# Expert input of a decoder step: the two products with the high weight as one 512-column matmul, halves added by VectorE

## The chip, the cores and the metric

One Trainium2 chip, one core of it. The metric is the device time of one execution in microseconds, from the first to the last instruction on the slowest (here the only) core, as the median of the runs.

## What is computed

One layer of a hybrid decoder for 256 prompt tokens and 32 sample tokens (T = 288 together, D_MODEL = 2048): an input projection, three attention branches, their output projection, and then a layer of product-key experts. The change lies in that last part. Its reference, cut to what matters:

```python
def peer_ffn(xn, w_q, keys, u, v):          # 16384 experts, 8 heads, 16 picks a head
    q = (tb @ w_q).reshape(nt, PEER_HEADS, 2, PEER_DK)
    sc = jnp.einsum('thcd,hcnd->thcn', q, keys)
    # top 16 of each half, top 16 of the 256 pairs, softmax: weights g, expert numbers eid
    act = jax.nn.gelu(jnp.einsum('thkd,td->thk', u[eid], tb), approximate=False)
    return jnp.einsum('thk,thkd->td', (g * act), v[eid])
```

## The kernel before

For 256 of the 288 tokens (DENSE) the kernel doesn't gather experts. It multiplies all 16384 rows of u with the tokens, takes gelu, weighs the result with a table that is zero where a token didn't pick the expert, and multiplies with v. The last 32 tokens (SPARSE) go by gathered rows: dots with rows of u, sums with rows of v.

Every product of f32 numbers is made of three products in a reduced 32-bit format: x = x_high + x_low and w = w_high + w_low, and the product is w_high x_high + w_high x_low + w_low x_high, all three summed in the same bank.

The stage of the change is the expert input, in `peer` (from line 2360). The 128 experts of a block are the columns of the weights, the contraction runs over D_MODEL in KT = 16 tiles of 128. BLOCKS = 128 blocks go through these steps, all engines at work on different blocks:

- DMA loads the block of u, 1 MB, half of it issued by SyncE once both halves of an earlier block are turned (`load_u`), half by ScalarE behind `high` (`load_quadrants`, line 2451). There are two buffers, and three from block 30 on (THIRD_FROM).
- VectorE transposes it in two half blocks (`turn`, line 2795). `half_block` does one such transpose and the dots of gathered rows due then. In the first third, half blocks are dealt out between the instructions of the top-16 search for three groups of tokens (`top16`, `worked`), in proportion to their cost. Later, `hot_rows` (lines 2905 and 2910) makes the operands of the weight table between the two halves.
- ScalarE copies each half to uT_high (`high`, line 2672), once PE is done with the block before last. GpSimd subtracts it for uT_low (`low_halves`, line 2645) and issues the gathers.
- PE runs `hidden(s, c)` (from line 2538): for each of the 16 tiles the high weight with x_high (line 2545) and with x_low (line 2546), then, after four-matmul pieces of the weight table (`spread`, line 2581), for each tile the low weight with x_high (line 2552). All 48 matmuls have 256 columns and sum into the first half of bank 4 or 5, by turns. The first one waits for `gelu_ready` of the block before last, which frees the bank.
- ScalarE takes gelu from the bank into a ring of four buffers (`gelu`, line 2681). SyncE stores it to DRAM (`store_gelu`, line 2480), three blocks behind the turned block.

The orders on each engine are written out by hand and all its instructions are in that order: a wait stops what is queued behind it. ScalarE does in its loop over m: `high(m + 1)`, what is due of the picks and of the weight table, `gelu(m)`. At blocks 44 and 64 PE turns picks and waits for ScalarE's copy of them. `after(n)` in a wait is a semaphore's start value plus n.

Behind block 127 comes the output stage (`four`, `output`, lines 2612 to 2614): 128 blocks of v, 24 matmuls of 512 columns each. VectorE weighs the gelu rows (`weigh`, line 2938, 2945, 2947) and makes the low half of v (`low_v`, line 2952). The gelu rows and the table come back from DRAM by `load_weights` (lines 2475 and 2476), the second of them behind the last `store_gelu`.

## Time and profile before

| what | value |
|---|---|
| runs | 3119.73, 3121.1, 3122.23 us; median 3121.1 us |
| span of the profiled execution (no other time is given for it) | 3122.4 us |
| instructions | 52270 |
| PE busy | 2977.9 us, 95% |
| weight loads (beside PE) | 2779.4 us, 89% |
| VectorE busy | 1834.2 us, 59% |
| ScalarE busy | 1266.4 us, 41% |
| GpSimd busy | 1023.3 us, 33% |
| DMA | 698.31 MB, mean 224 GB/s |

A matmul's duration is modelled and overlaps the next one's, so paces are read from starts, or from how many start in a stretch. Starts are us from the span's start. PE is the matmul row, PEld the weight loads, DVE is VectorE, ACT ScalarE, POOL GpSimd, SP SyncE; a q behind the name is the engine's queue where it issues DMAs. "banks" are the PSUM banks. The clock is the share of TensorE's full clock that was granted.

### The profile page before, as it was taken

How to read it: one execution, taken by the hardware profiler on the slowest of the kernel's cores; microseconds unless marked ns; L12 is line 12 of the kernel's file. 1: busy time of each engine (PE TensorE's matmuls, PEld its weight loads, DVE VectorE, ACT ScalarE, POOL GpSimd, SP SyncE). 2: the span in 40 equal slices, each digit the busy share in tenths (PEclk: the TensorE clock that was granted, in tenths of full speed). 3: DMA queues.
4: the chain of work that ended last, by engine and by line, in shares of the span. 5: the costliest groups of instructions: out<-in, count | busy, mean ns of one | idle time of the engine just before them, and what ended most of it. 6: DMA issues, size and time to landing. Idle time of an engine off the chain costs nothing. (4 is left out here: it accounts for less than half of the span.)

```text
span 3122.4 us, 52270 instructions
## 1 busy us (share of the span) xinstructions
PE 2977.9 (95%) x20998; PEld 2779.4 (89%) x20998; DVE 1834.2 (59%) x2568; ACT 1266.4 (41%) x1399; POOL 1023.3 (33%) x549
## 2 busy tenths in 40 slices
PE   7999999898989979998999999999999999999997
PEld 6999999887888869997999999999998888888886
DVE  5444444375221145645468999877784577767764
ACT  5322233345533454433344444445553333333332
POOL 0000000134644420024057889777775011111000
PEclk9999999999999989999999999999999999999999
DMA  7555544575675646666768999999999788888754
GB/s 233 182 167 167 166 161 161 166 226 163 186 250 182 222 141 190 200 206 168 153 159 191 241 242 236 255 287 289 273 266 358 257 319 312 304 297 306 289 199 174
DMA packets 449277, 698.31 MB, mean 224 GB/s; under 512 B 30981, under 2 KB 345765, under 8 KB 421582
## 3 DMA queue, kind: packets, MB, share of 16 engines
q1 hardware_dynamic: 398622, 553.81, 57.7%
q10 hardware_dynamic: 41296, 75.53, 8.8%
q0 software_dynamic: 9216, 67.11, 5.7%
q8 instruction: 84, 1.38, 0.2%
q14 instruction: 59, 0.48, 0.0%
HBM read 629.24 MB, written 63.72 MB: 222 GB/s over the span
## 5 line engine op out<-in xcount | busy, mean ns | idle before, releaser
L2645 POOL TENSOR_TENSOR peer_uT_low<-peer_uT,peer_uT_high 128x1024 fp32r<-128x1024 f32 x256 | 615.6, 2427 | 255.3 <-ACT peer_uT_high L2672 254.7
L1054 POOL TENSOR_TENSOR gate_low<-gate_raw,gate_high 128x512 fp32r<-128x512 f32 x192 | 257.9, 1368 | 878.9 <-ACT gate_high L1005 878.5
L2545 PE MATMUL banks<-x_high,peer_uT_high 128*128 128x256 f32 x2048 | 493.1, 283 | 5.1 <-ACT peer_picks_T L2704 5.1
L2546 PE MATMUL banks<-x_low,peer_uT_high 128*128 128x256 f32 x2048 | 489.1, 280 | 0.0
L2545 PEld LDWEIGHTS banks<-x_high,peer_uT_high 128*128 128x128 f32 x2048 | 386.6, 189 | 5.8 <-ACT peer_uT_high L2672 2.9
L2546 PEld LDWEIGHTS banks<-x_low,peer_uT_high 128*128 128x128 f32 x2048 | 385.8, 188 | 0.0
L257 PE MATMUL banks<-x_high,win_high 128*128 128x288 f32 (+1 forms) x1312 | 349.3, 296 | 0.0
L258 PE MATMUL banks<-x_low,win_high 128*128 128x288 f32 (+1 forms) x1312 | 348.7, 295 | 0.0
L227 ACT ACTIVATE win_high<-win_raw 128x2048 fp32r<-128x2048 f32 x84 | 160.8, 1914 | 332.5 <-DVEq L220 319.2
L2672 ACT ACTIVATE peer_uT_high<-peer_uT 128x1024 fp32r<-128x1024 f32 x256 | 260.5, 1053 | 59.2 <-DVE peer_uT L2795 58.8
L2795 DVE STREAM_TRANSPOSE peer_uT<-peer_u 128x1024 f32<-128x1024 f32 x192 | 233.8, 1229 | 82.9 <-DMA peer_u<-in_peer_u_dram 56.8
L2552 PE MATMUL banks<-x_high,peer_uT_low 128*128 128x256 f32 x2048 | 263.8, 282 | 0.0
L233 DVE TENSOR_TENSOR win_low<-win_raw,win_high 128x2048 fp32r<-128x2048 f32 x84 | 192.4, 2291 | 116.8 <-ACT win_high L227 116.8
L2552 PEld LDWEIGHTS banks<-x_high,peer_uT_low 128*128 128x128 f32 x2048 | 250.2, 189 | 0.0
L258 PEld LDWEIGHTS banks<-x_low,win_high 128*128 128x128 f32 x1312 | 247.2, 188 | 0.1
L257 PEld LDWEIGHTS banks<-x_high,win_high 128*128 128x128 f32 x1312 | 246.5, 188 | 0.3
L1068 PE MATMUL banks<-x_high,gate_high 128*128 128x288 f32 x768 | 222.7, 311 | 22.2 <-POOL gate_low L1054 15.0
L2653 POOL DMA_INDIRECT peer_area<-in_peer_v_dram,peer_expert_row x32 | 61.9, 1935 | 472.7 <-DVE peer_area L2920 471.7
L2720 ACT ACTIVATE peer_uT_high<-peer_u 128x2048 fp32r<-128x2048 f32 x64 | 122.8, 1919 | 227.8 <-PE banks L2614 201.3
L1069 PE MATMUL banks<-x_low,gate_high 128*128 128x288 f32 x768 | 213.7, 300 | 0.0
L2612 PE MATMUL banks<-x_high 128*128 128x512 f32 x512 | 201.0, 393 | 12.2 <-DVE x_low L2952 12.2
L2720 ACT ACTIVATE x_high<-peer_area 128x2048 fp32r<-128x2048 f32 x64 | 122.7, 1919 | 219.2 <-PE banks L2614 217.0
(395 smaller groups left out, 6502.0 us busy)
## 6 DMA issues: line engine op xcount, KB each, us to landing
win_raw<-in_w_in_dram SPq DMA_DIRECT2D x38, 2048.0 KB, 8.1
peer_u<-in_peer_v_dram SPq DMA_DIRECT2D x64, 1024.0 KB, 5.6
peer_area<-in_peer_v_dram SPq DMA_DIRECT2D x64, 1024.0 KB
gate_raw<-in_w_in_dram SPq DMA_DIRECT2D x96, 512.0 KB, 5.0
peer_u<-in_peer_u_dram SPq DMA_DIRECT2D x192, 256.0 KB
peer_u<-in_peer_u_dram ACTq DMA_DIRECT2D x192, 256.0 KB
w_raw<-in_w_up_ret_dram SPq DMA_DIRECT2D x8, 2048.0 KB, 9.0
w_raw<-in_w_out_dram SPq DMA_DIRECT2D x8, 2048.0 KB, 8.4
```

The source lines that it names most:

```text
L257: pe.matmul(out, w, xh[:, k, :], start=(k == 0), stop=False)
L258: pe.matmul(out, w, xl[:, k, :], start=False, stop=False)
L1054: pool.tensor_tensor(self.low[:, p % 2, c, :, :], self.raw[:, p % 4, :, c * P:(c + 1) * P], self.high[:, p % 2, c, :, :], ALU.subtract).th ...
L1068: pe.matmul(out, high, self.xh[:, 4 * q + k, :], start=(q == 0 and k == 0), stop=False)
L1069: pe.matmul(out, high, self.xl[:, 4 * q + k, :], start=False, stop=False)
L2545: pe.matmul(out, UH[:, c, k, :], XH[:, k, 0:DENSE], start=(k == 0), stop=False)
L2546: pe.matmul(out, UH[:, c, k, :], XL[:, k, 0:DENSE], start=False, stop=False)
L2552: last = pe.matmul(out, UL[:, c, k, :], XH[:, k, 0:DENSE], start=False, stop=(k == KT - 1))
L2645: pool.tensor_tensor(UL[:, m % 2, part, :], UT[:, m % 2, part, :], UH[:, m % 2, part, :], ALU.subtract).then_inc(low, 1)
L2672: act.activation(UH[:, m % 2, part, :], UT[:, m % 2, part, :], ACT.Copy).then_inc(uT_high, 1)
L2720: act.activation(VH[n % 4], V[n % 4], ACT.Copy).then_inc(v_high, 1)
L2795: dve.transpose(UT[:, m % 2, b * HALF:(b + 1) * HALF, :].rearrange("p c (E e) -> p E c e", E=4), u_block(m)[:, :, cols].rearrange("p E (c ...
```

## The change

The two products with the high weight become one matmul of 512 columns. x_high and x_low now lie in one tensor, and the matmul's moving operand is 256 columns of each. Its result is the whole bank: in the first half the product with x_high, in the second that with x_low. The low weight's product is still summed into the first half.

So the halves have to be added before gelu. ScalarE copies the second half to SBUF (`cross`), VectorE adds the first half from the bank and writes the ring of gelu rows (`add_cross`), and ScalarE takes gelu in place. VectorE's sum of block m stands in `half_block`, right ahead of the second transpose of block m + 3 (HIDDEN_BEHIND); the last three sums stand behind all of VectorE's work of the stage, ahead of the first `weigh`. The wait for the stored gelu row moves from ScalarE to that sum. PE's wait for a free bank is now for the sum of the block before last. ScalarE does gelu one block later: its loop ends with `cross(m)`, `gelu(m - 1)`.

```diff
-            XH = tensor(right, "right", "x2_high", [P, KT, T], F32R)
-            XL = tensor(right, "right", "x2_low", [P, KT, T], F32R)
+            X2 = tensor(right, "right", "x2", [P, 2, KT, T], F32R)
+            XH, XL = X2[:, 0], X2[:, 1]
...
-TURNS_AHEAD, GATHERS_AHEAD = 2, 4
+TURNS_AHEAD, GATHERS_AHEAD, HIDDEN_BEHIND = 2, 4, 3
...
+        CROSS = st.sb("cross_products", [P, 2, DENSE])
...
                     out = PS[:, 4 + c, 0:DENSE]
-                    pe.wait_ge(gelu_ready, after(m - 1))
+                    parts = PS[:, 4 + c, :].rearrange("p (x t) -> p x t", x=2)
+                    pe.wait_ge(hidden_added, after(m - 1))
                     for k in range(KT):
                         if k % HALF == 0:
                             pe.wait_ge(uT_high, after(m * 2 + k // HALF + 1))
-                        pe.matmul(out, UH[:, c, k, :], XH[:, k, 0:DENSE], start=(k == 0), stop=False)
-                        pe.matmul(out, UH[:, c, k, :], XL[:, k, 0:DENSE], start=False, stop=False)
+                        pe.matmul(parts, UH[:, c, k, :], X2[:, :, k, 0:DENSE], start=(k == 0), stop=False)
...
+                def cross(m):
+                    act.wait_ge(hidden_done, after(m + 1))
+                    act.wait_ge(hidden_added, after(m - 1))
+                    act.activation(CROSS[:, m % 2, :], PS[:, 4 + m % 2, DENSE:2 * DENSE], ACT.Copy).then_inc(cross_copied, 1)
+
                 def gelu(m):
-                    act.wait_ge(hidden_done, after(m + 1))
-                    act.wait_ge(ge_stored[m % 4], after(16 * (m // 4)))
-                    act.activation(GE[:, m % 4, :], PS[:, 4 + m % 2, 0:DENSE], ACT.Gelu).then_inc(gelu_ready, 1)
+                    act.wait_ge(hidden_added, after(m + 1))
+                    act.activation(GE[:, m % 4, :], GE[:, m % 4, :], ACT.Gelu).then_inc(gelu_ready, 1)
...
-                    gelu(m)
+                    cross(m)
+                    if m:
+                        gelu(m - 1)
+                gelu(BLOCKS - 1)
...
+                def add_cross(m):
+                    dve.wait_ge(cross_copied, after(m + 1))
+                    dve.wait_ge(ge_stored[m % 4], after(16 * (m // 4)))
+                    dve.tensor_tensor(GE[:, m % 4, :], PS[:, 4 + m % 2, 0:DENSE], CROSS[:, m % 2, :], ALU.add).then_inc(hidden_added, 1)
+
                 def half_block():
                     h = next(halves)
+                    if h % 2 == 1 and h // 2 >= HIDDEN_BEHIND:
+                        add_cross(h // 2 - HIDDEN_BEHIND)
                     turn(h)
...
+                for m in range(BLOCKS - HIDDEN_BEHIND, BLOCKS):
+                    add_cross(m)
                 weigh(0)
```

## Rows read from the trace of the kernel before

**Rows 1.** The page, first section: busy us, share of the span, instructions

```profile
PE 2977.9 (95%) x20998; PEld 2779.4 (89%) x20998; DVE 1834.2 (59%) x2568; ACT 1266.4 (41%) x1399; POOL 1023.3 (33%) x549
```

**Rows 2.** The chain of waits, 1660 to 1690 us: start us, us, what

```profile
1667.30 1.88 PE banks L2552 x16
...
1684.24 1.88 PE banks L2552 x16
```

**Rows 3.** Groups by shape, 1580 to 2410 us: count, busy us, mean ns, idle before

```profile
L2645 POOL TENSOR_TENSOR peer_uT_low<-peer_uT,peer_uT_high 128x1024 fp32r<-128x1024 f32 x256 | 615.6, 2427 | 255.3 <-ACT peer_uT_high L2672 254.7
...
L2795 DVE STREAM_TRANSPOSE peer_uT<-peer_u 128x1024 f32<-128x1024 f32 x192 | 233.8, 1229 | 82.9 <-DMA peer_u<-in_peer_u_dram 56.8 <-POOL peer_uT_low L2645 25.5
```

**Rows 4.** Windows of VectorE, blocks 16-30, 30-44: us, busy, clock, DMA share, GB/s

```profile
1678.00:1757.00 79.00, 67.36 (x174) 1.00 0.86 207
1757.00:1832.00 75.00, 72.97 (x125) 1.00 0.97 254
```

**Rows 5.** VectorE's waits, 1584 to 1678, 1678 to 1757, 1832 to 1909: us, times, longest

```profile
DVE peer_uT L2795 <- DMA peer_u<-in_peer_u_dram: 13.7, 7, 7.5
...
DVE peer_uT L2795 <- DMA peer_u<-in_peer_u_dram: 13.8, 8, 2.8
...
DVE peer_uT L2795 <- POOL peer_uT_low L2645: 9.5, 6, 4.4
```

**Rows 6.** Windows, PE alone, output stage: us, busy (matmuls), clock, DMA, GB/s

```profile
2500.00:2600.00 100.00, 100.00 (x442) 1.00 0.84 307
```

**Rows 7.** Groups by shape of VectorE and ScalarE, whole span: count, busy, mean ns

```profile
L2070 DVE TENSOR_TENSOR up_mix<-banks,up_gates 128x288 f32<-128x288 f32 x16 | 7.3, 455 | 41.8 <-ACT up_gates L2058 34.1 <-PE banks L263 7.6
...
L559 ACT ACTIVATE Z<-banks 128x256 f32<-128x256 f32 x8 | 3.1, 383 | 40.3 <-PE banks L668 40.3
```

**Rows 8.** Transposes from 1580 us on (count, ns), and timeline near 1707 us

```profile
L2795 DVE STREAM_TRANSPOSE peer_uT<-peer_u x42: 1198/1232/1248, 1584.0 to 1707.4; 128x1024 f32<-128x1024 f32 x42
...
1706.66 2.04 PE L2552 MATMUL banks<-x_high,peer_uT_low 128*128 128x256 f32 x16
...
1707.38 1.25 DVE L2795 STREAM_TRANSPOSE peer_uT<-peer_u 128x1024 f32<-128x1024 f32 x1
```

**Rows 9.** Timeline near block 37: start us, us, engine, line, count

```profile
1797.01 2.04 PE L2552 MATMUL banks<-x_high,peer_uT_low 128*128 128x256 f32 x16
...
1801.79 1.24 DVE L2795 STREAM_TRANSPOSE peer_uT<-peer_u 128x1024 f32<-128x1024 f32 x1
```

**Rows 10.** Timeline near block 59

```profile
1924.52 2.04 PE L2552 MATMUL banks<-x_high,peer_uT_low 128*128 128x256 f32 x16
...
1929.30 1.24 DVE L2795 STREAM_TRANSPOSE peer_uT<-peer_area 128x1024 f32<-128x1024 f32 x1
```

**Rows 11.** Timeline near block 83, VectorE and PE: in brackets the idle time before

```profile
2077.74 1.25 DVE L2795 STREAM_TRANSPOSE peer_uT<-peer_area 128x1024 f32<-128x1024 f32 x1 [6.00 <-DMA peer_area<-in_peer_u_dram]
...
2084.84 1.24 DVE L2795 STREAM_TRANSPOSE peer_uT<-peer_area 128x1024 f32<-128x1024 f32 x1
...
2083.11 1.16 PE L2581 MATMUL banks<-peer_keys_T_and_hot_rows 128*128 128x128 f32 x8 [2.78 <-DVE peer_keys_T_and_hot_rows L2910]
2084.02 0.36 PE L2545 MATMUL banks<-x_high,peer_uT_high 128*128 128x256 f32 x1
```

**Rows 12.** Timeline at the end of the stage, 2381 to 2411 us

```profile
2381.68 4.75 POOL L2645 TENSOR_TENSOR peer_uT_low<-peer_uT,peer_uT_high 128x1024 fp32r<-128x1024 f32 x2 [0.90 <-ACT peer_uT_high L2672]
...
2385.56 1.49 DVE L2938 TENSOR_TENSOR peer_area<-peer_area 128x256 f32<-128x256 f32 x2 [8.21 <-DMA peer_area<-peer_weights]
...
2389.49 2.04 PE L2552 MATMUL banks<-x_high,peer_uT_low 128*128 128x256 f32 x16
...
2392.82 0.48 SPq L2476 DMA_DIRECT2D peer_area<-peer_weights  x1
...
2408.75 0.77 PE L2612 MATMUL banks<-x_high 128*128 128x512 f32 x1 [6.32 <-DVE x_low L2952]
...
2410.17 0.63 PE L2612 MATMUL banks<-x_high 128*128 128x512 f32 x1
```

More of the change, by code:

```diff
@@ L336, in decoder_step_kernel @@
                 output_projection(nc, G, MH, ML, hT, area, moved, keys_loaded, gain_loaded, w_out, w_q)
-            XH = tensor(right, "right", "x2_high", [P, KT, T], F32R)
-            XL = tensor(right, "right", "x2_low", [P, KT, T], F32R)
+            X2 = tensor(right, "right", "x2", [P, 2, KT, T], F32R)
+            XH, XL = X2[:, 0], X2[:, 1]
             norm_and_queries(nc, G, area, hT, XH, XL, moved, spilled, gain_loaded, w_q)
             left.close()
-            peer(nc, G, area, XH, XL, spilled, keys_loaded)
+            peer(nc, G, area, X2, spilled, keys_loaded)
 def constants(const):
@@ L2357, in spread_at, with peer @@
     return range(spread_before(m), spread_before(m + 1))
-def peer(nc, G, area, XH, XL, spilled, keys_loaded):
+def peer(nc, G, area, X2, spilled, keys_loaded):
     A, PS, ident, C, S, O = (G[k] for k in ("A", "PS", "ident", "C", "S", "O"))
+    XH, XL = X2[:, 0], X2[:, 1]
     GR = 2 * PEER_HEADS
@@ L2431, in peer @@
             "second_ready", "first_ready", "placed", "weights_ready", "weights_stored")
-        turned, uT_high, low, hidden_done, gelu_ready, iota_ready, xrows_moved = st.sems(
-            "turned", "uT_high", "uT_low", "hidden_done", "gelu_ready", "iota_ready", "xrows_moved")
+        turned, uT_high, low, hidden_done, cross_copied, hidden_added, gelu_ready, iota_ready, xrows_moved = st.sems(
+            "turned", "uT_high", "uT_low", "hidden_done", "cross_copied", "hidden_added", "gelu_ready", "iota_ready", "xrows_moved")
         u_loaded = st.sems(*(f"u_loaded{r}" for r in range(4)))
```

## The prediction

> **What bounds the kernel now.** The page's first section gives the order of the engines: PE is busy in 95% of the span [rows 1]. The change touches one stage, the expert input, whose 128 blocks run from 1588 us to 2391 us, so I read that stage. The chain of waits shows it as PE alone: a block's low products come every 5.647 us (1667.30 to 1684.24 is three blocks [rows 2]), which is 48 matmuls at 117.65 ns with no gap. So PE is the bound, and what PE saves is saved, as long as its suppliers keep up. They are close behind. The groups of the stage give the cost of the suppliers per block [rows 3]: POOL 256 x 2.43 us, that is 4.86 us a block; VectorE two transposes of 1.23 us, and beside them all the top-16 picking, in the first 66 blocks. By the windows, VectorE is busy in 67.4 of 79 us, then in 73.0 of 75 us [rows 4]. Its waits are for the DMA of u up to block 30 (13.7, 13.8 us) and only from block 46 on for POOL (9.5 us) [rows 5]. So for the first 44 blocks nothing holds VectorE back but its own work and its loads. That it costs no time now is because it runs ahead of PE by a lead that is allowed to shrink.
>
> **The matmuls.** Removed are 2048 pairs of 256-column matmuls with the same weights, added 2048 matmuls of 512 columns. A pair takes 2 x 117.65 = 235.3 ns [rows 2]. The next stage issues matmuls of just this width with new weights each: 442 in 100 us, 226.2 ns [rows 6]. The moving operand is now read in two pieces of 256; nothing in the trace shows that as a cost, and I take 226.2. Saving 9.1 ns x 2048 = 18.6 us, or 0.145 us a block. Bounds: 235.3 ns (no saving) and 213.3 ns (512 columns at the granted 2.4 GHz, 45 us). The row is the same width and type, so I take it.
>
> The trace's 117.65 ns is 11 ns above 256 columns at the granted 2.4 GHz. The Trainium skill (TensorE: Matmul & The Clock Gate, section "Wait — 56ns, not 53.3ns?") states a fixed 2.5 ns over the columns for every warm matmul; by that a pair would go from 218.3 to 215.8 ns and the change could save 5 us only. The rows at either width disagree with it.
>
> **ScalarE.** Per block a copy of 128x256 out of a bank is added; such a copy takes 383 ns [rows 7]. Gelu stays, now from SBUF. ScalarE's queue then has, after a block's end on PE: copy, gelu of the block before, the two high halves. The high halves come 0.4 us later, and POOL's halves behind them. POOL's halves for block 127 end at 2381.68 + 4.75 = 2386.43, and PE starts the low products at 2389.49 [rows 12]: 3.1 us of cover for 0.4. Where PE waits for ScalarE itself, at the two hand-overs of the picks, the 0.4 us shows: +0.8 us.
>
> **VectorE.** 128 additions of 256 columns with one operand in a bank. The nearest row is a sum of 288 columns with one operand in a bank, 455 ns [rows 7]; by columns alone 256 take 404 ns. I take 0.42 us between the two. In the first 66 blocks it has no room for them, see above.
>
> **The new wait, which decides.** Before, PE started block m once gelu of block m-2 was done, by ScalarE, which is always there in time. After, it needs the sum of block m-2, and that stands in VectorE's queue right ahead of the second transpose of block m+1. So PE's block B-1 can't start until VectorE has come to the second transpose of block B, plus 0.42 for the sum and 0.1 to wake: half a microsecond. Before, it only had to have block m itself turned. I count transposes on VectorE, and PE's blocks in the same way by their 16 low products, to see where it stood. The 42nd transpose (block 20, second half) starts at 1707.38; the low products of PE's block 19 start at 1706.66 and take 1.88, so with 5.65 a block it started at 1702.9: VectorE is 4.5 us too late for the new order [rows 8]. By the same count, block 37 (76th) at 1801.79 against block 36 on PE at 1798.9: 2.9 us too late [rows 9]. Block 59 (120th) at 1929.30 against block 58 at 1926.4: again 2.9 us [rows 10]. PE will be stopped in each, so its shift P against before is at least D + 3.4 at the last two, where D is VectorE's own delay by the new sums.
>
> D: between blocks 3 and 37 there are 35 sums, 14.7 us if all count, 0 if all fall into its DMA waits of 27 us. Loads are issued behind the second transpose, and u has two buffers up to block 30, so every other block a sum is inside the loop that the load closes, and the other one falls into the wait; from block 30 VectorE is full. So (27 / 2 + 8) x 0.42 = 9, less what the waits early on hide, about 3: D = 6. P = 9.4 at block 36. From there PE recovers 0.145 a block as long as it isn't stopped, and VectorE, which waits for POOL there, is tied to it: P = 7.5 at block 52, D with it. Then seven sums (2.9) without a wait ahead of block 59: D = 10.5, P = 14.
>
> From block 58: 70 blocks x 0.145 = -10; the hand-over of the picks is in the 0.8 above. In the second half (blocks 66 on) VectorE has a lead of more than 0.6 us nearly everywhere, enough for the sum. One pattern breaks it: a late load of u holds VectorE's queue 6.0 us, and the second transpose of block 83 comes at 2084.84, 0.8 us after PE's block 82 started at 2084.02 [rows 11]. The sum now stands behind that load: +1.3 there, and about 1 each for the two other times that the weight table is stored, +3.
>
> A stop of PE also costs clock. After 2.78 us idle [rows 11] and after 6.32 us idle [rows 12] the matmuls behind it come at half the pace (three of 512 columns in 1.42 us, 2408.75 to 2410.17). Two of the new stops are 4 us long in one piece; I put 1 us on each, since PE waits on VectorE there anyway: +2.
>
> **End of the stage.** Before, weigh, split and subtraction of the first v block ran on VectorE beside PE's block 127 (2385.56 and after), and PE went on at once [rows 12]. Now they are queued behind the sum of block 127: some 0.9 + 1.49 + 0.43 + 0.69 + 2.29, about 6 us after PE's end. That gap is mostly not new: before PE stood for 6.32 us two v blocks later, for the second load of weights, which is issued after the last gelu (2392.82). The last gelu now ends 1.2 us later, and the two v blocks in front of it fit in the same time. +1.3.
>
> Sum on the profiled execution: P 14 + 0.8 - 10 + 3 + 2 + 1.3 = +11. Its span is 3122.4 us, no other time is given for it, and it stands 1.3 above the median of the runs, 3121.1. So 3132 us for the median. A difference under 0.2% (6 us) I count as none, about what a measurement of this kernel can tell.
>
> **The rivals.**
> (a) VectorE has room: the sums fall into the DMA waits and D is 0. Then P is 3.4 at block 36, 1.5 at block 52, 4.9 at block 58 and the total is about +1: 3122. For it: 27 us of waits. Against: 73.0 of 75 busy. With D between 0 and 3 it stays within 0.2%.
> (b) The order isn't binding at all, because a PE that is stopped once lets VectorE lead from there on, and wide matmuls pay in full: -18.6 + 1.3 + 3, 3107. It needs VectorE to keep 5.5 us a block with sums in it, so that after the first stop of 4.5 us none follows: some -10, 3111.
> (c) Worse than forecast: loads decide. All 35 sums count (D = 14.7, P = 18 at block 36), and the stores of the gelu rows, which leave a block later, meet the weight table in SP's queue, so that VectorE's sum waits for a row of the buffer: +18 to +30, 3139 to 3151. It decides where a store takes more than two blocks.
> (d) The wide matmul isn't faster than its pair: 235.3 instead of 226.2 ns, everything else as forecast: 3149, or 3135 where VectorE bounds the first half anyway. The rows of the next stage speak against it. The Trainium skill's rule above would be near this case.
>
> **How the numbers follow.** Forecast (+5 to +16) 0.45, (a) 0.25, (b) 0.17, (c) 0.08, (d) 0.05. The likeliest case alone is 3126 to 3138. Of the forecast's cases a small part is inside 0.2%, so faster 0.18, same 0.27, slower 0.55. The range leaves out a tenth on either side: 3108 to 3146.
>
> **What would show it.** Right: PE's matmuls of 512 columns 226 ns apart in a stretch without stops, 5.50 us a block; PE idle in front of the first matmul of a block with VectorE's sum as the releaser, most in blocks 18 to 44 and 56 to 62, some 20 to 30 us in all; VectorE almost without idle time there; the last blocks of the stage with hardly any. Wrong: the sum of 256 columns well under 0.4 us; blocks at 5.50 us already between 20 and 40 (then (a) or (b)); blocks spaced over 5.64 us without a wait (then (d)). The forecast falls if PE's idle time on that wait is under 12 us.

## The result, and the profile after

The changed kernel takes 3166.09 us (median of four runs, 3163.62 to 3170.87), the kernel before in the same comparison 3120.41 (3119.63 to 3122.23). The ratio is 1.0146 with a 95% interval of 1.0131 to 1.0160: slower by 46 us. The profiled execution took 3167.94 us, its span is 3166.2 us, 43.8 over the 3122.4 of before. The forecast was 3132 us, with a range of 3108 to 3146. The sign is right, the size is not: the measured time lies 20 us above the range.

The first section of the page, busy us, share of the span and instructions [rows 1]:

```profile
PE 2983.6 (94%) x18950; PEld 2689.3 (85%) x18950; DVE 1871.0 (59%) x2696; ACT 1302.1 (41%) x1527; POOL 1022.0 (32%) x549
```

PE has 2048 matmuls less. VectorE has 128 instructions and 37 us more: 128 sums at 0.41 us are 52 us, and the rest of its work sums to 15 us less in this profile. The engines' totals say little; the waits say where the time is. First PE's waits in the stage, 1580 to 2470 us of the changed kernel: engine, line, waited for, us in total, times, longest:

```profile
PE banks L2583 <- ACT peer_area L2717: 21.6, 3, 8.4
PE banks L2548 <- DVE peer_gelu L2813: 16.8, 10, 2.9
PE banks L2548 <- ACT peer_picks_T L2710: 5.7, 2, 3.0
PE banks L2614 <- DVE peer_uT_low L2968: 5.2, 1, 5.2
PE banks L2614 <- DVE x L2968: 4.9, 1, 4.9
...
```

The same view of the kernel before, 1580 to 2420 us:

```profile
PE banks L2612 <- DVE x_low L2952: 6.3, 1, 6.3
PE banks L2581 <- DVE peer_keys_T_and_hot_rows L2910: 5.2, 3, 2.8
...
PE banks L2581 <- ACT peer_area L2711: 1.1, 2, 0.9
```

The second line of the changed kernel's is the wait that the forecast counted on: the first matmul of a block (L2548) waits for VectorE's sum (L2813). The first line is the surprise. At three places the weight table's matmuls (L2583) wait for ScalarE's L2717, a step that used to cost 1.1 us. L2717 takes a finished piece of the table out of its bank (`keep`), and at those three places a new group of tokens begins, so that the old table must have gone to DRAM first.

To see where the shift arises I took the start of each block on PE in both profiles. The stage itself begins 3.2 us earlier in the changed kernel's profile, a variation of what lies ahead of it, so I count from the stage's first block:

| stretch | shift gained, us | what it is |
|---|---|---|
| blocks 0 to 66 | +17.0 | eight stops for the sum (15.2, of which 13.0 are idle time), a block at half the clock behind three of them (5.0), the picks (0.6), less 66 faster blocks (4.0) |
| blocks 66 to 127, ordinary blocks | -2.7 | the wide matmul, 0.06 us a block, less small stops |
| blocks 81 to 83, 95 to 99, 108 to 112 | +5.4, +7.5, +7.9 | the three hand-overs of the weight table |
| blocks 124 to 126 | +4.3 | a stop for the sum, which is queued behind a late load of u, and a block at half the clock |
| from block 127 on | +7.6 | the change to the output stage |
| total | +47.0 | |

**The stops for the sum.** Of the 16.8 us of waits for the sum in the stage, most lie ahead of block 66; the same view from 1580 to 1970 us:

```profile
PE banks L2548 <- DVE peer_gelu L2813: 13.0, 8, 2.9
```

The timeline of PE in the changed kernel, start, us, instruction, and in brackets the idle time ahead of it:

```profile
1708.04 5.54 PE L2548 MATMUL banks<-x,peer_uT_high 128*128 128x512 f32 x16 [2.87 <-DVE peer_gelu L2813]
1713.41 2.05 PE L2554 MATMUL banks<-x,peer_uT_low 128*128 128x256 f32 x16
1715.30 3.86 PE L2548 MATMUL banks<-x,peer_uT_high 128*128 128x512 f32 x16
1719.00 2.05 PE L2554 MATMUL banks<-x,peer_uT_low 128*128 128x256 f32 x16
```

Two things are to be seen. PE stood for 2.87 us, and then 16 matmuls of 512 columns took 5.54 us instead of 3.86. The granted clock tells why; the windows of PE over a part of each of the two blocks (us, busy and matmuls, clock, DMA share, GB/s):

```profile
1708.10:1711.50 3.40, 3.40 (x10) 0.64 0.38 42
1715.40:1718.90 3.50, 3.50 (x17) 1.00 1.06 240
```

The first mean, 0.64, is a mixture of the two levels, 1.2 and 2.4 GHz. It happened behind the three longest of the eight stops, ahead of blocks 19, 34 and 56 (2.87, 2.59 and 2.42 us idle); with it they cost 4.7, 4.4 and 4.2 us.

Not every such stop has a halved clock behind it. PE also waits for the picks, ahead of block 44. Here is that stop in the changed kernel, and then in the profile of the experiment table_first, whose program does the same up to this point:

```profile
1857.55 3.97 PE L2548 MATMUL banks<-x,peer_uT_high 128*128 128x512 f32 x16 [3.00 <-ACT peer_picks_T L2710]
```

```profile
1860.18 5.52 PE L2548 MATMUL banks<-x,peer_uT_high 128*128 128x512 f32 x16 [3.00 <-ACT peer_picks_T L2710]
```

The same 3.00 us of idle time, and behind it 16 matmuls in 3.97 us at a granted clock of 1.00 once, in 5.52 us at 0.67 the other time. So the length of a stop doesn't decide it, and a single profile can differ from the next by such blocks.

**The pace between stops.** The block is read between the starts of its low products, 1713.41 to 1719.00: 5.59 us, where [rows 2] had 5.65 and the forecast 5.50. The low products themselves keep 117.65 ns, so the wide matmul takes 231.6 ns, not 226.2.

**A hand-over.** Three views of the first one belong together. SyncE's queue in the changed kernel:

```profile
2070.87 0.34 SPq L2482 DMA_DIRECT2D gelu<-peer_gelu  x1
2071.26 0.95 SPq L2497 DMA_DIRECT2D peer_weights<-peer_area  x2
...
2076.45 0.34 SPq L2482 DMA_DIRECT2D gelu<-peer_gelu  x1
2076.84 1.36 SPq L2497 DMA_DIRECT2D peer_weights<-peer_area  x2
```

And in the kernel before:

```profile
2052.62 0.43 SPq L2480 DMA_DIRECT2D gelu<-peer_gelu  x1
2053.09 0.92 SPq L2495 DMA_DIRECT2D peer_weights<-peer_area  x2
...
2059.61 0.44 SPq L2480 DMA_DIRECT2D gelu<-peer_gelu  x1
2060.09 0.98 SPq L2495 DMA_DIRECT2D peer_weights<-peer_area  x2
```

In either, the store of the table follows a store of a gelu row by 0.4 us: it is queued behind it in SyncE's order of instructions. The gelu row now comes one block later, and so does the table, although no edit names the table. With the 13 us shift of this place taken off, the first table store is at 2058.3 instead of 2053.1, the second at 2063.8 instead of 2060.1. The chain of waits of the changed kernel follows it on:

```profile
2076.84 0.86 SPq L2497
...
2077.74 22.76 DMA peer_weights<-peer_area
...
2100.59 1.03 ACT peer_area L2717
...
2101.76 2.04 PE banks L2583 x8
```

ScalarE waited 11.09 us for this store ahead of L2717, where before it waited 2.73 us, and PE stood for 8.42 us ahead of 2101.76 behind it. The store's own time in flight is longer too: 22.8 us from the end of its issue, and before 17.8, from the end of its issue at 2061.07 to ScalarE's copy at 2078.83.

**The end of the stage.** VectorE in the changed kernel:

```profile
2428.11 0.42 DVE L2813 TENSOR_TENSOR peer_gelu<-banks,peer_cross_products 128x256 f32<-128x256 f32 x1 [5.16 <-ACT peer_cross_products L2683]
...
2430.43 4.48 DVE L2968 TENSOR_TENSOR peer_uT_low<-peer_u,peer_uT_high 128x2048 fp32r<-128x2048 f32 x2
2446.12 0.76 DVE L2954 TENSOR_TENSOR peer_area<-peer_area 128x256 f32<-128x256 f32 x2 [11.21 <-DMA peer_area<-peer_weights]
```

PE's block 127 ends at 2427.67. The work for the first v block stands behind the last sum, and PE starts the output stage 5.2 us later. Two v blocks on it stops again for the second load of weights, 4.90 us, until 2450.42. From the end of block 127 to there are 22.75 us; before, from 2391.57 to 2408.75 [rows 12], 17.2. The load is issued 1.8 us after the end instead of 1.25, and is in flight 16.25 us instead of 11.61.

### The profile page after: what moved, and what is told of

The parts are those of the page before. It is cut to its first block, busy times and chain, and to the rows that moved or that the text cites. A ratio compares the mean times of both kernels' runs of the same rounds, so it can differ in the third digit from the quotient of the medians.

```text
span 3166.2 us, 48558 instructions
## 1 busy us (share of the span) xinstructions
PE 2983.6 (94%) x18950; PEld 2689.3 (85%) x18950; DVE 1871.0 (59%) x2696; ACT 1302.1 (41%) x1527; POOL 1022.0 (32%) x549
## 4 chain that ended last, share of the span: by engine, by line
PE 40%; DMA 5%; DVE 3%; issue 1%; ACT 1%; POOL 0%; ACTq 0%; SPq 0%; DVEq 0%
PE banks L2548 11%; PE banks L2614 7%; PE banks L2616 7%; PE banks L2615 7%; PE banks L2554 6%; DMA peer_u<-in_peer_u_dram 2%; PE banks L2583 2%; DMA peer_weights<-peer_area 1%; DVE peer_uT L2804 1%; DMA peer_area<-peer_weights 1%; DMA peer_area<-in_peer_v_dram 0%; POOL peer_uT_low L2647 0%; DVE x L2968 0%; PE banks L2567 0%; PE banks L2635 0%
## 5 line engine op out<-in xcount | busy, mean ns | idle before, releaser
L2548 PE MATMUL banks<-x,peer_uT_high 128*128 128x512 f32 x2048 | 508.9, 401 | 22.6 <-DVE peer_gelu L2813 16.8
L2548 PEld LDWEIGHTS banks<-x,peer_uT_high 128*128 128x128 f32 x2048 | 382.5, 192 | 106.4 <-issue 15.1
L2554 PEld LDWEIGHTS banks<-x,peer_uT_low 128*128 128x128 f32 x2048 | 257.2, 189 | 8.7
L2554 PE MATMUL banks<-x,peer_uT_low 128*128 128x256 f32 x2048 | 263.7, 282 | 0.0
L2726 ACT ACTIVATE x<-peer_area 128x2048 fp32r<-128x2048 f32 x64 | 122.8, 1919 | 226.6 <-PE banks L2616 218.9
L2614 PE MATMUL banks<-x 128*128 128x512 f32 x512 | 201.7, 394 | 11.0 <-DVE x L2968 11.0
L2614 PE MATMUL banks<-peer_uT_high,peer_act_high 128*128 128x512 f32 x512 | 200.7, 392 | 5.2 <-DVE peer_uT_low L2968 5.2
L2615 PE MATMUL banks<-x 128*128 128x512 f32 x512 | 201.4, 393 | 0.0
```

The costliest lines, as they stand in the source:

```text
L2548: pe.matmul(parts, UH[:, c, k, :], X2[:, :, k, 0:DENSE], start=(k == 0), stop=False)
L2554: last = pe.matmul(out, UL[:, c, k, :], XH[:, k, 0:DENSE], start=False, stop=(k == KT - 1))
L2614: pe.matmul(out, high, VH[slot][:, cols], start=first, stop=False)
L2615: pe.matmul(out, rest, VH[slot][:, cols], start=False, stop=False)
L2726: act.activation(VH[n % 4], V[n % 4], ACT.Copy).then_inc(v_high, 1)
```

## The experiments

Shifts are again counted from the stage's first block, on the profiles; medians and ratios are those of the runs beside the kernel before. "Hand-overs" are the three of the weight table.

### The wide matmul alone

Only the matmul is changed; the bank's second half, the product with x_low, is not added, and this product is left out of the output. Everything else is as before.

```diff
-  pe.matmul(out, UH[:, c, k, :], XH[:, k, 0:DENSE], start=(k == 0), stop=False)
-  pe.matmul(out, UH[:, c, k, :], XL[:, k, 0:DENSE], start=False, stop=False)
+  pe.matmul(parts, UH[:, c, k, :], X2[:, :, k, 0:DENSE], start=(k == 0), stop=False)
```

> The change's wide matmul alone, on the kernel before: the 512-column matmul into the whole bank, and then gelu of the first half as before, by ScalarE, with the waits and the queues of before. Left out: the product of the high weight with x_low. Theory 'two pieces': the moving operand in two pieces of 256 costs about 5 ns a matmul, so a pair of 235.3 ns becomes one of 231.6 ns as in the changed kernel, 3.7 x 2048 = 7.6 us less than before: 3113 us, no stops of PE in the picks. Rival 'disturbed': the matmul is as fast as those of the output stage (226.2 ns), and in the changed kernel the new reads of the banks by ScalarE and VectorE slowed it: 18.6 us less, 3102 us.

Measured: 3123.66 against 3123.32 us, ratio 0.9998 (0.9987 to 1.0009). No gain is seen, and the interval has no room for the 7.6 us that were expected. Its timeline gives the pace without any sum in the kernel:

```profile
1882.58 3.86 PE L2548 MATMUL banks<-x,peer_uT_high 128*128 128x512 f32 x16
1886.28 2.05 PE L2554 MATMUL banks<-x,peer_uT_low 128*128 128x256 f32 x16
1888.16 3.86 PE L2548 MATMUL banks<-x,peer_uT_high 128*128 128x512 f32 x16
```

1882.58 to 1888.16, 5.58 us a block as in the changed kernel: 231.6 ns belong to the matmul. And the 0.06 us a block that are left don't arrive in the first half: PE, now faster, has to wait for halves that were there in time before, and longer for the picks. Its waits in the stage:

```profile
PE banks L2548 <- ACT peer_picks_T L2706: 7.8, 2, 5.4
...
PE banks L2548 <- ACT peer_uT_high L2674: 2.9, 2, 2.6
```

It stands 2.6 us at 1712 us and 5.4 instead of 2.7 for the picks, and behind both the clock was halved (eight wide matmuls in 3.38 us instead of 2.02, then 16 in 5.33 instead of 3.86). The shift is +5.7 at block 66, where the matmuls alone would give -4.0. From there to block 127 it falls to +0.6: in the second half the saving does arrive. The end is at +2.9, and this profile is 4 us above the median of its runs.

### Why 231.6 ns: one piece, address, bank

The first two runs start from mm_alone: the high weight is multiplied with 512 other, adjacent columns of x_high, so that both of its products are replaced; the second differs from the first in where the columns start. The third, in the kernel before, orders the output stage's matmuls by the weight, so that each goes to another bank than the one before it. This also names one weight four times in a row, but the weight loads stay one per matmul. In this order:

```diff
+  pe.matmul(PS[:, 4 + c, :], UH[:, c, k, :], xh[:, k * DENSE:k * DENSE + 2 * DENSE], start=(k == 0), stop=False)
...
+  pe.matmul(PS[:, 4 + c, :], UH[:, c, k, :], xh[:, k % 8 * 512:k % 8 * 512 + 512], start=(k == 0), stop=False)
...
+  for weight, v, begin, end in ((high, VH, first, False), (rest, VH, False, False), (high, VL, False, last)):
+      for j in range(4):
+          ins = pe.matmul(PS[0:r, 4 * i + j, :], weight, v[slot][:, j * 512:(j + 1) * 512], start=begin, stop=end)
```

> As the run before it, but the moving operand is 512 adjacent columns (of x_high alone, so the products are of other columns). Theory 'two pieces': 226 ns a matmul, 3102 us, 11 us less than with two pieces. Rival: the two pieces cost nothing and something else makes 231.6 ns in this stage (the weights' place, the u loads): same time as the run before it, 3113 us.

> As mm_one_piece, but the 512 columns start at multiples of 512 columns of the same tensor (2 KB apart, as the v rows in the output stage) instead of multiples of 256; the products are of other columns. Theory 'address': the pace of 232 ns comes from where the moving columns start; now 226.5 ns. Rival 'same bank': 16 matmuls in a row sum into one bank, against three in the output stage; still 231 to 233 ns.

> The kernel before with the output stage's 24 matmuls of 512 columns per block in another order: all four banks with one weight, then the next weight, so that no two matmuls in a row sum into the same bank. For the pace of the wide matmul: 16 in a row into one bank take 231 to 233 ns apart in the expert input, three in a row 226.5 ns here. Theory 'same bank': a matmul behind one into the same bank starts later; alternating banks take 216 to 222 ns, up to 30 us less: 3095 us. Rival: it is not the bank, 226.5 ns as before, 3121 us.

Measured: mm_one_piece 3129.93 against 3123.32 us, ratio 1.0012 (1.0001 to 1.0024), 233.3 ns; mm_steps, a single run, 3124.13 us, 233.3 ns; output_by_bank 3123.45 against 3123.19 us, ratio 1.0005 (0.9995 to 1.0015), its pace as in [rows 6], 442 in 100 us. The timeline of mm_one_piece:

```profile
1883.77 3.89 PE L2548 MATMUL banks<-x,peer_uT_high 128*128 128x512 f32 x16
1887.50 2.03 PE L2554 MATMUL banks<-x,peer_uT_low 128*128 128x256 f32 x16
```

1883.77 to 1887.50 are 3.73 us for 16. The operand in two pieces is not what costs 5 ns, nor its start address, and in the output stage staying in a bank doesn't make a matmul slower. What does stays open. Within a block of the changed kernel the starts lie 225 to 237 ns apart, by nearly the same pattern over the 16 tiles in most blocks; mm_alone has this pattern too.

### The place of the wait alone

No sum; VectorE only passes a semaphore on in the place where the sum would stand, and PE waits for that.

```diff
+  pe.wait_ge(passed, after(m - 1))
...
+  if h % 2 == 1 and h // 2 >= 3:
+      dve.wait_ge(gelu_ready, after(h // 2 - 2))
+      dve.sem_inc(passed, 1)
```

> The kernel before, and PE waits for VectorE's place in its queue as in the changed kernel: VectorE raises a semaphore ahead of the second transpose of block m+3, once gelu of block m is done, and PE starts block m+2 only then. No sum, no wide matmul, no change in SyncE's queue. Theory 'place': PE stops near blocks 19, 35 and 57 where VectorE trails, at least 4.5 us in all and 1.6 us for the clock after each stop, and PE, at its pace of before, recovers none of it: +6 to +8 us by block 66, some 2 to 4 more at the late loads: 3130 us. Rival 'price': it is the sums that cost the time in the first half, the place alone costs under 3 us: 3123 us.

Measured: 3127.77 against 3123.32 us, ratio 1.0006 (0.9997 to 1.0016). In the profile the shift is +3.4 at block 66, +8.6 at block 127, +9.1 at the end; the runs show less: the medians are 4 us apart, the ratio says 2 us, and its interval includes none. The stop is ahead of block 19, where the forecast's count put it, and 1.6 us long; it is the only one on this wait. Of the +3.4, 1.4 us are a block at half the clock behind the stop for the picks, a stop that the kernel before has as well. The rest of the shift comes at the weight table's hand-overs, where the wait for `keep` is 5.8 us instead of 1.1. The order by itself is cheap as long as VectorE's work doesn't grow.

### The price of the sums alone

First with both operands in SBUF, because no bank is free of other use at that time; nobody reads the result.

```diff
+  SPARE = st.sb("spare", [P, 2, DENSE])
...
+  if h % 2 == 1 and h // 2 >= 3:
+      dve.tensor_tensor(SPARE[:, 0, :], SPARE[:, 1, :], SPARE[:, 1, :], ALU.add).then_inc(spared, 1)
```

> The kernel before, and VectorE does one more sum of 256 columns at the place where the changed kernel has it, on a spare buffer that nobody reads or waits for. Theory 'price': VectorE has no room in the first 44 blocks, so the transposes come later by up to 6 us and PE stops for ScalarE's high halves near blocks 20 and 36: +3 to +10 us, 3129 us. Rival 'fits': the sums fall into the waits for loads: within 1 us of before.

Measured: 3177.31 against 3124.27 us, ratio 1.0170 (1.0153 to 1.0187), more than the whole change. It is not a test of the price, since the sum is not the same instruction any more. Its group in the stage (count, busy us, mean ns, idle before):

```profile
L2808 DVE TENSOR_TENSOR peer_spare<-peer_spare 128x256 f32<-128x256 f32 x125 | 133.2, 1065 | 0.3
```

1065 ns instead of 408. The timeline of VectorE and of GpSimd shows the longest one:

```profile
1906.91 7.15 DVE L2808 TENSOR_TENSOR peer_spare<-peer_spare 128x256 f32<-128x256 f32 x1
...
1906.67 7.10 POOL L2645 TENSOR_TENSOR peer_uT_low<-peer_uT,peer_uT_high 128x1024 fp32r<-128x1024 f32 x3
```

The sum stands about as long as three subtractions of GpSimd in a row, 1906.67 to 1913.77, and ends 0.3 us behind them. The Trainium skill (SBUF — State Buffer, section "Who interferes with whom") says that a VectorE instruction with two SBUF inputs contends with a GpSimd instruction that reads SBUF, while one with at most one SBUF input, outside VectorE's two-port modes, doesn't. This case agrees, by these rows and by the next run, where the mean is 406 ns instead of 1065.

So the same again with one operand in a bank (the constant iota, read from PSUM in two pieces of 128):

```diff
+  dve.tensor_tensor(SPARE[:, 0, :].rearrange("p (x n) -> p x n", x=2), PIOTA.unsqueeze(1).to_broadcast([P, 2, P]), SPARE[:, 1, :].rearrange("p (x n) -> p x n", x=2), ALU.add).then_inc(spared, 1)
```

> The kernel before, and at the place where the changed kernel has its sum VectorE adds 256 columns of a bank (the iota that lies there) to a spare buffer; nobody reads the result or waits for it. It differs from sums_alone in one thing: one operand is in a bank, as in the changed kernel, and not both in SBUF, where the sums took 1.07 us on average and up to 7 us behind a subtraction of GpSimd. Theory 'shared way to SBUF': these take 0.39 to 0.42 us each, as in the changed kernel, and then 'price' decides: VectorE comes later in the first 66 blocks, +3 to +10 us, 3129 us. Rival 'fits': 0 to 1 us.

Measured: 3140.15 against 3124.66 us, ratio 1.0051 (1.0039 to 1.0063). Group and waits of PE in the stage:

```profile
L2809 DVE TENSOR_TENSOR peer_spare<-banks,peer_spare 128x256 f32<-128x256 f32 x125 | 50.7, 406 | 0.5 <-DVE peer_picks L2894 0.4
```

```profile
PE banks L2545 <- ACT peer_picks_T L2704: 9.3, 2, 6.0
...
PE banks L2545 <- ACT peer_uT_high L2672: 4.3, 6, 2.6
```

406 ns is the price of the change's sum (408). The shift is +15.8 at block 66, +19.2 at block 127, +20.2 at the end. Here no new wait exists: PE stops because the picks come later (6.0 us in one stop, 2.7 before) and because the transposed halves do. Of the 26 us of sums up to block 66 some 16 arrived, in spite of VectorE's 27 us of DMA waits [rows 5]. A part of the 16 is clock: behind the two stops for the picks a block took 8.2 and 8.3 us from start to start, where the same blocks took 5.75 before.

### Place and price together

The unread sum of sums_bank, behind a wait for gelu of the block whose sum it stands for, with PE waiting for it; the matmuls stay as before.

```diff
+  pe.wait_ge(spared, after(m))
...
+  dve.wait_ge(gelu_ready, after(h // 2 - 2))
```

> The kernel before with the unread bank sums of sums_bank and PE's wait for them as in the changed kernel, no wide matmul and nothing changed on SyncE. Theory 'parts add': the sums alone gave +15 us, the wait for the place alone +4 us by the runs (9 us by the profile of the stage), so +18 to +24 us, 3145 us. Rival 'interplay': a sum that is late and waited for costs more than both alone, +30 us or more, 3155 us.

Measured: 3148.66 against 3123.19 us, ratio 1.0078 (1.0065 to 1.0090). The shift is +22.4 at block 66, +28.8 at block 127, +27.7 at the end, against 9.1 + 20.2 = 29.3 for the two alone. By the profiles they add. By the medians the two alone are 4.5 and 15.5 us over the kernel before, 20.0 together, and this kernel is 25.5 over it, a little more than the 18 to 24 expected; so some microseconds that only the two together cost can't be excluded. Its stops are ahead of much the same blocks as the changed kernel's:

```profile
PE banks L2546 <- DVE peer_spare L2811: 12.9, 8, 4.8
PE banks L2582 <- ACT peer_area L2712: 5.3, 2, 3.8
```

Against it the changed kernel has 15.4 us more in the hand-overs (5.3 us of waiting for `keep` here, 21.6 there), 8.7 more from block 127 on and 3.6 more at block 124; it has 5.4 less up to block 66, and 3 less between, where its wide matmul counts.

### The stores one block later, alone

```diff
 def store_gelu(m):
-    sp.wait_ge(gelu_ready, after(m + 1))
+    sp.wait_ge(gelu_ready, after(min(m + 2, BLOCKS)))
```

> The kernel before with one wait changed: SyncE's store of a gelu row waits until the gelu of the next block is done, as it has to in the changed kernel. No sum, no wide matmul. Theory 'queue': the stores of the weight table are queued behind it on SyncE, so each of the three hand-overs of the table to the next token block comes a block (5.6 us) later, and PE, which before stood 2.8 us at the first of them, stands that much longer: +14 to +18 us, 3137 us. Rival 'load': those stops grew because VectorE's sum is queued behind late loads of u; then this kernel is as before, 3121 us.

Measured: 3139.02 against 3123.32 us, ratio 1.0046 (1.0029 to 1.0063). One number in a kernel that is otherwise the one before, and +16 us. SyncE's queue, where the second store of the table was at 2060.09 before (this profile's stage begins 1.1 us later), and PE's waits:

```profile
2063.98 0.34 SPq L2480 DMA_DIRECT2D gelu<-peer_gelu  x1
2064.37 2.49 SPq L2495 DMA_DIRECT2D peer_weights<-peer_area  x2
```

```profile
PE banks L2581 <- ACT peer_area L2711: 13.0, 3, 5.4
...
PE banks L2612 <- DVE x_low L2952: 4.8, 1, 4.8
...
PE banks L2612 <- DVE peer_uT_low L2952: 4.1, 1, 4.1
```

The shift is zero up to block 81, +9.9 at block 113, and +13.9 at the end: the three hand-overs and the end of the stage, with a second stop of 4 us there, and nothing else. 13.0 of the changed kernel's 21.6 us are reproduced. What the others need beside the late stores isn't shown by a run; the late VectorE is the likely part, since place_and_price has 5.3 us of this wait without late stores.

### The table ahead of the gelu row

The converse, in the changed kernel: SyncE stores the table first.

```diff
-    if m >= 3:
-        store_gelu(m - 3)
     k, r = divmod(m - SPREAD_FROM - SPREAD_ACTIVE - 2, SPREAD_SPAN)
     if 0 <= k < TOKEN_BLOCKS and r < 2:
         ...
+    if m >= 3:
+        store_gelu(m - 3)
```

> The changed kernel, with the two parts of the weight table's stores put ahead of the store of the gelu row in SyncE's loop; nothing else. Theory 'queue': the hand-overs of the table at blocks 81, 95 and 109 get back the block that they lost, 5 us and some clock each: 14 to 18 us less than the changed kernel, 3150 us, and PE's waits for ScalarE's copy of the table fall from 21.6 us to some 6. Rival 'load': those stops are late loads behind the table's stores, which stay: under 4 us less, 3163 us.

Measured: 3159.79 against 3124.27 us (3150.0 to 3163.47), ratio 1.0112 (1.0089 to 1.0135). The hand-overs fall from 20.8 to 6.0 us in the profile and the wait for `keep` from 21.6 to 6.4 us; the first half came out at +24 instead of +17 in that profile, though this edit changes nothing there (the stop ahead of block 13 is 4.6 us instead of 1.6, and a halved clock also follows it and both stops for the picks), and the runs spread over 13 us, so the net gain, 1.0112 against 1.0146, is some 11 us, under the 14 to 18 expected, and uncertain by several. The same edit in the kernel before:

> The kernel before, with only the order on SyncE changed: table stores ahead of the gelu row's store. There gelu is done by then, so theory 'queue' expects nothing or the time of one store's issue (0.5 us) on each hand-over: 0 to -2 us, 3121 us. If the stops at the hand-overs were bound by that order even before, -5 us.

Measured: 3123.83 against 3123.19 us, ratio 1.0001 (0.9992 to 1.0010). Before, the table wasn't late.

### The sum at another place

Half a block earlier on VectorE, ahead of the first transpose of block m + 3:

```diff
-  if h % 2 == 1 and h // 2 >= HIDDEN_BEHIND:
+  if h % 2 == 0 and h // 2 >= HIDDEN_BEHIND:
```

> The changed kernel with the sum of block m ahead of the first transpose of block m+3 instead of the second: half a block earlier in VectorE's queue, and in front of the wait for the load of u. Theory 'place': most of the eight stops go, 10 to 18 us less than the changed kernel, 3152 us; the three stops at the table's hand-over stay. Rival 'price alone': under 5 us less, 3163 us.

Measured: 3150.17 against 3124.66 us, ratio 1.0081 (1.0068 to 1.0095). That is 20 us less over the kernel beside it than the change has, more than the 10 to 18 expected. The stops for the sum fall to 9.0 us, the shift at block 66 to +11.4 from +17.0. The hand-overs shrink only a little: PE stands 7.51, 6.54 and 3.76 us there, instead of 8.42, 7.90 and 5.32. A whole block earlier (HIDDEN_BEHIND = 2):

> The changed kernel with VectorE's sum two blocks behind its transposes instead of three (HIDDEN_BEHIND = 2). PE's block then needs VectorE at the second transpose of that same block, a whole block later than now, but VectorE can't run further ahead than PE's last finished block. Theory 'place': the eight stops of PE before a sum (15 us, and 5 us of half clock) go; 12 to 20 us less than the changed kernel, 3150 us. Rival 'VectorE waits': the time that it now stands for PE's products comes back as later transposes and loads: 3166 us or more.

Measured: 3183.6 against 3124.66 us, ratio 1.0193 (1.0180 to 1.0207). PE's waits in the stage:

```profile
PE banks L2583 <- ACT peer_area L2717: 34.1, 13, 10.1
PE banks L2583 <- DVE peer_keys_T_and_hot_rows L2926: 8.1, 9, 1.7
...
PE banks L2548 <- DVE peer_gelu L2813: 6.0, 5, 2.2
```

The stops for the sum are nearly gone, 6.0 us, and the shift at block 66 is +13.5. But in the second half (1980 to 2440 us) VectorE now waits for ScalarE's copy of a block that PE has only just ended:

```profile
DVE peer_gelu L2813 <- ACT peer_cross_products L2683: 99.3, 45, 5.9
```

In the changed kernel this wait is 20.6 us there. What is queued behind it is the operands of the weight table, and PE stops for the table 22 times in all (13 and 9). Of the three places tried, half a block earlier is the best.

### A bank freed by ScalarE alone

ScalarE copies both halves out in one instruction, PE waits for that copy, and VectorE adds in SBUF, in its own time.

```diff
-  pe.wait_ge(hidden_added, after(m - 1))
+  pe.wait_ge(cross_copied, after(m - 1))
...
-  act.activation(CROSS[:, m % 2, :], PS[:, 4 + m % 2, DENSE:2 * DENSE], ACT.Copy).then_inc(cross_copied, 1)
+  act.activation(RING[:, a:b + 1:b - a, :], PS[:, 4 + m % 2, :].rearrange("p (x t) -> p x t", x=2), ACT.Copy).then_inc(cross_copied, 1)
...
-  dve.tensor_tensor(GE[:, m % 4, :], PS[:, 4 + m % 2, 0:DENSE], CROSS[:, m % 2, :], ALU.add).then_inc(hidden_added, 1)
+  dve.tensor_tensor(GE[:, m % 4, :], GE[:, m % 4, :], CROSS[:, m % 2, :], ALU.add).then_inc(hidden_added, 1)
```

> The changed kernel, but ScalarE copies both halves of the bank in one instruction (512 columns), the first into the ring of gelu rows, PE waits for that copy as it waited for gelu before, and VectorE adds in place from SBUF at the same place in its queue. The sum stays, PE's wait for VectorE's place is gone. Theory 'place with price': the eight stops before a sum (15 us in the profile of the changed kernel, and 5 us of half clock behind three of them) are gone and PE may trail VectorE as before; a stop or two for late high halves comes in their place: 12 to 18 us less, 3151 us. Rival 'price alone': VectorE's load is what stops PE, wherever PE waits: under 6 us less, 3162 us.

> Both of the last two edits together. If they are two separate causes, their gains add: some 30 us less than the changed kernel, 3135 us. If one only uncovers the other, the gain is that of the larger alone, 3150 us.

Measured: bank_freed 3216.88 against 3124.27 us, ratio 1.0305 (1.0288 to 1.0322); freed_table_first, with the table's store ahead as well, 3211.69 us, ratio 1.0280 (1.0263 to 1.0297). The 3151 and 3135 us expected are missed by 66 and 77 us, for a reason that neither theory nor rival had. PE's wait for the sum is gone, and the sum costs 3.5 times as much:

```profile
L2814 DVE TENSOR_TENSOR peer_gelu<-peer_gelu 128x256 f32<-128x256 f32 x128 | 183.1, 1431 | 12.0 <-ACT peer_gelu L2685 8.7 <-issue 3.0
```

128 x 1.02 us is 131 us more of VectorE, the engine that had no room. That is the behaviour of sums_alone, met by a design that looked better on paper.

### Half a block earlier and the table first

Both edits, sum_first_half and table_first, in the changed kernel:

> The changed kernel with both remedies: the sum ahead of the first transpose, and the weight table's stores ahead of the gelu row's store. Alone they brought 16 us and some 6 to 14 us. If the queue and VectorE's place are separate causes: 3138 us, the stops at the table's hand-overs back at 5 to 7 us in all; what is left over the kernel before is the price of the sums. If they overlap: 3147 us.

Measured: 3140.16 against 3123.19 us, ratio 1.0058 (1.0045 to 1.0071), 26 us better than the change as made and the best version that has wide matmuls and adds all three products; still 17 us slower than the kernel before, near the 15.5 us that the sums cost by themselves. PE's waits:

```profile
PE banks L2548 <- DVE peer_gelu L2813: 7.7, 7, 3.5
...
PE banks L2583 <- ACT peer_area L2717: 4.5, 6, 2.3
```

Both lines fall, each by its own edit, so the stops and the hand-overs are separate causes. The shift is +9.6 at block 66, +11.1 at block 127, +16.9 at the end.

### The ledger

By the profiles from the stage's start to the end: wide matmul +2.9, price of the sums +20.2, place of the wait +9.1, late stores +13.9. The sum is 46.1; the changed kernel has +47.0. This agreement is in part luck, since single profiles vary by several microseconds and those of the wide matmul and of the place each lie 4 us above the median of their runs. By the medians the same four are 0.3, 15.5, 4.5 and 15.7 us, 36 together, against 46 for the change; with place_and_price (25.5) for the two middle ones they are 41.5. So 4 to 10 us are not accounted for by single causes. The stop at block 124 is one candidate: its 4.3 us appear in none of the four.

## Why the prediction was wrong in size

**What held.** The forecast's main mechanism is there: PE stops at the first matmul of a block with VectorE's sum as the releaser, ahead of blocks 19, 34 and 56 most of all; the count of transposes [rows 8 to 10] had put it at 19, 36 and 58. The sum was taken at 0.42 us and has a mean of 0.41. The clock falls behind such a stop, three times up to block 66, some 1.7 us each. PE's idle time on this wait is 16.8 us, under the 20 to 30 forecast and over the 12 at which the forecast was to fall. The largest chance, 0.55, lay on slower.

**Term by term**, forecast against measured:

| term | forecast | measured |
|---|---|---|
| shift at block 66 (14 + 0.8, less the first wide blocks; clock 2) | +15.6 | +17.0 |
| the wide matmul from there on | -9 | -3.7 |
| hand-overs of the weight table | +3 | +20.8 |
| late load at block 124 | 0 | +4.3 |
| end of the stage | +1.3 | +7.6 |
| not assigned | | +1.0 |
| total | +11 | +47.0 |

**The step that failed** is the one on the second half: "The sum now stands behind that load: +1.3 there, and about 1 each for the two other times that the weight table is stored, +3." It looked only at VectorE's queue. The step that was moved also moved the last one behind it: gelu a block later, hence `store_gelu` a block later, and SyncE's queue is one order in which the table's stores stand right behind it. The forecast had the late stores in rival (c), but as a matter of the ring of gelu rows, and not of what else is behind them in the queue, and gave that 0.08. stores_late shows it by itself: +10 in the hand-overs and +4 at the end, from one number. In table_first, with the stores back in their place, the hand-overs are 15 of the 20.8 us shorter.

**The wide matmul.** "The row is the same width and type, so I take it" was wrong by more than half of the gain: 231.6 instead of 226.2 ns, a saving of 0.06 us a block instead of 0.145. The operand's two pieces and its start address are not the reason, nor by the output stage the bank; it stays open. By the fixed 2.5 ns over the columns that the Trainium skill states (TensorE: Matmul & The Clock Gate, section "Wait — 56ns, not 53.3ns?") the matmul would take 215.8 ns, an estimate from that figure; the trace disagrees, with 231.6. And the price was not the only error: in mm_alone the saving of 0.06 us a block brings no gain in the whole time, since in the first half PE waits for halves and picks instead. The forecast said "what PE saves is saved, as long as its suppliers keep up", and then counted the saving in full from block 58 on.

**Right for the wrong reason.** The 14 us at block 58 were made of D, the delay of VectorE, at 10.5, and 3.4 for the place. In the runs the place alone gives 3.4 at block 66 as well, but 1.4 of it are clock behind the picks, and the sums alone, without the new wait, give 15.8, by later picks and later halves. D let half the sums fall into DMA waits, and was probably too small; how much of the 15.8 is VectorE's delay and how much clock wasn't separated. (The working also has a slip: 9.4 less 16 blocks at 0.145 is 7.1 at block 52, not 7.5.) Place and price together have 22.4 there (place_and_price), the halved clock included; less 4.0 for 66 faster blocks that is 18.4. The changed kernel has 17.0 in one profile and 24.0 in that of table_first, which does the same up to there. That 15.6 comes so near to 17.0 is therefore partly luck. The clock behind the stops was taken as 2 and came to 5.

**The end.** "That gap is mostly not new" held that the wait for the first v block and that for the second load would overlap. They came one after the other, 5.2 and 4.9 us, because the load was issued later and flew 4.6 us longer. Why it flew longer wasn't tried; in stores_late, where it leaves later too, it took 14.8 us. The stop at block 124 is not a consequence of the late table: table_first has it too, +4.2 us. It goes where the sum stands ahead of the late load (sum_first_half, half_and_table). VectorE waited for this load before the change too, 6.8 us, without a stop of PE; why it lands later against PE's blocks in the changed kernel is open.

## What to carry to other kernels

When a step is made later, follow it through every queue that its result passes, to whatever stands behind its consumer there: the item that the forecast missed by most is a DMA that no edit touches, late because the one ahead of it in SyncE's order waits for a gelu. Where the busiest engine is fed by one that is busy 97% of the time, as VectorE is here in blocks 30 to 44, a small saving on the first can bring nothing (mm_alone), and much of the work added to the second is paid for (16 of 26 us in sums_bank); find that out by making the saving and the added work alone. Keep one operand of a VectorE sum in its bank while GpSimd works in SBUF: the copy that was to free PE from VectorE made this kernel some 50 us slower. And read a shift of a few microseconds from more than one profile.

## What the runs showed of the hardware beyond what was expected

- A sum of 256 columns on VectorE takes 0.41 us with one operand in a bank and a mean of 1.07 to 1.43 us with both in SBUF beside GpSimd's subtractions, up to 7.15 us.
- A 512-column matmul with new weights each took 231.6 to 233.3 ns in this stage and 226 to 227 ns in the next, with the operand in one piece or two, at other start addresses, and (in the next stage) whether the bank stays or changes.
- After stops of PE of 2.9, 2.6 and 2.4 us a block took 7.3 us instead of 5.6, and the granted clock was 0.64 in most of the first of them; after stops of 3.0 and 2.7 us in the same profile it took 5.7. In the profile of table_first the same two stops were followed by 7.2 and 7.1 us, and in that of sum_first_half a stop of 3.4 us by 5.7. Stops of 1.2 to 1.6 us had none of this in these profiles.
- The store of the weight table at the first hand-over was in flight for 22.8 us, and for 17.8 us before; the runs don't show why.
